# Reading the moving operands of the weight-stream matmuls from the last element to the first

## The reference

```python
h = rmsnorm(x, g_mix)
proj = h @ w_in                  # q, k, v, forget logits, LRU x, LRU gate, memory q, 3 x 2048 merge-gate logits
mk, mv = split(rmsnorm(mem, g_mem) @ w_mem_kv)
...                              # y_fox (causal attention), y_lru (gated recurrence), y_mem (cross-attention)
y_d = einsum('bsnc,ncd->bsnd', branches, w_branch)
x = x + sum(sigmoid(gate_logits + b_gate) * y_d) @ w_out
up = causal_conv3(rmsnorm(x, g_ffn) @ w_ffn_up)
u_act, u_val = split(up)
return x + (gelu(u_act) * u_val) @ w_ffn_down
```

## Time and profile before

| | |
|---|---|
| median of 2 runs | 1644.3 us (1644.13 to 1644.46) |
| the profiled execution's own time | 1643.98 us |
| its span, first to last instruction | 1642.2 us |
| mean granted TensorE clock | 0.998 |
| PE, matmuls | 1628.4 us busy, 8560 instructions |
| PEld, weight loads | 1392.5 us, 8560 |
| DVE | 1050.9 us, 1257 |
| ACT | 870.2 us, 1192 |
| POOL | 25.3 us, 30 |
| DMA | 309.58 MB, mean 189 GB/s |

### The profile page before, as it was taken

One profiled execution on the slowest core, in us unless ns is written; L12 is line 12 of the kernel. 1 busy time (PEld: TensorE's weight loads), 2 busy tenths in 40 slices (PEclk: granted clock), 3 DMA queues, 4 the chain that ended last, 5 costly groups with the idle time before them and its releaser, 6 DMA issues.

```text
span 1642.2 us, 24812 instructions
## 1 busy us (share of the span) xinstructions
PE 1628.4 (99%) x8560; PEld 1392.5 (85%) x8560; DVE 1050.9 (64%) x1257; ACT 870.2 (53%) x1192; POOL 25.3 (2%) x30
## 2 busy tenths in 40 slices
PE   9999999999999999999999999999999999999999
PEld 7778888778888888888888888888888888888887
DVE  6755578656657565564755777777777777544443
ACT  7565667356554545445445655555555555433332
POOL 0000021000000000000000000000000000000000
PEclk9999999999999999999999999999999999999999
DMA  9544455655456556555565556555556555665663
GB/s 347 177 158 153 148 170 195 238 198 167 162 172 192 192 179 193 190 189 185 186 195 182 168 188 204 186 181 195 179 181 202 191 181 190 202 207 192 205 205 116
DMA packets 85280, 309.58 MB, mean 189 GB/s; under 512 B 9832, under 2 KB 10352, under 8 KB 84976
## 3 DMA queue, kind: packets, MB, share of 16 engines
q1 hardware_dynamic: 83952, 303.14, 55.7%
q0 software_dynamic: 1136, 5.78, 1.0%
q10 hardware_dynamic: 144, 0.01, 0.0%
HBM read 306.78 MB, written 2.11 MB: 188 GB/s over the span
## 4 chain that ended last, share of the span: by engine, by line
PE 94%; DVE 2%; DMA 2%; ACT 1%; SPq 0%; issue 0%; ACTq 0%; DVEq 0%
PE psG L359 90%; DMA raw<-w_units 2%; PE psM L359 2%; DVE W L1016 1%; PE psM L444 0%; ACT W L661 0%; DVE normed L1054 0%; PE psM L597 0%; DVE X L1200 0%; PE psM L480 0%; DVE x_n L1296 0%; ACT fox_square L690 0%; PE psM L478 0%; DVE dec_u L1163 0%; ACT L804 0%
## 5 line engine op out<-in xcount | busy, mean ns | idle before, releaser
L1016 DVE TENSOR_TENSOR W<-raw,W 128x1024 fp32r<-128x1024 f32 x566 | 686.6, 1225 | 390.8 <-ACT W L661 388.3
L359 PE MATMUL psG<-X,W 128*128 128x512 f32 (+1 forms) x4864 | 853.1, 337 | 0.0
L359 PEld LDWEIGHTS psG<-X,W 128*128 128x128 f32 x4864 | 741.5, 188 | 108.4
L661 ACT ACTIVATE W<-raw 128x1024 fp32r<-128x1024 f32 x566 | 590.5, 1055 | 402.4 <-PE psG L359 384.7
L359 PE MATMUL psG<-W,hidden 128*128 128x512 f32 x1056 | 239.5, 389 | 0.0
L359 PEld LDWEIGHTS psG<-W,hidden 128*128 128x128 f32 x1056 | 198.2, 188 | 41.0
L359 PE MATMUL psG<-W,X 128*128 128x512 f32 x768 | 180.5, 394 | 0.0
L359 PEld LDWEIGHTS psG<-W,X 128*128 128x128 f32 x768 | 144.5, 189 | 30.3 <-issue 0.4
L669 ACT ACTIVATE low<-psG 128x512 f32<-128x512 f32 x100 | 59.9, 599 | 153.6 <-PE psG L359 153.6
L359 PE MATMUL psG<-Y,W 128*128 x768 | 134.4, 337 | 0.0
L359 PEld LDWEIGHTS psG<-Y,W 128*128 128x128 f32 x768 | 117.0, 188 | 17.1
(11 more groups left out here) (191 smaller groups left out, 551.2 us busy)
## 6 DMA issues: line engine op xcount, KB each, us to landing
raw<-w_units SPq DMA_DIRECT2D x566, 512.0 KB, 3.8
xs<-xT SPq DMA_DIRECT2D x4, 512.0 KB, 8.4
x_tok<-x_rows POOLq DMA_DIRECT2D x1, 2048.0 KB, 13.7
mem_raw<-first_data SPq DMA_DIRECT2D x3, 512.0 KB, 4.8
mem_raw<-memT SPq DMA_DIRECT2D x3, 512.0 KB, 7.5
out<-x_tok POOLq DMA_DIRECT2D x3, 512.0 KB, 4.2
lru_rg<-w_rg POOLq DMA_DIRECT2D x8, 128.0 KB, 4.0
c_all<-c_rows POOLq DMA_DIRECT2D x1, 1024.0 KB, 8.1
```

The source lines that it names most:

```text
L359: return nc.tensor.matmul(*a, skip_group_check=True, **kw)
L661: nc.scalar.activation(W[:, s, :, 0], raw[:, s], ACT.Copy).then_inc(hi_done, 1)
L1016: V.tensor_tensor(W[:, s, :, 1], raw[:, s], f32(W[:, s, :, 0]), ALU.subtract).then_inc(lo_done, 1)
```

## The change

Every matmul of a unit reads its moving operand from the last column to the first. In the narrow groups the activations keep their layout, so the results come out in reverse order and are written backwards into `psG`, which puts each at its old place. In the wide groups the host lays out the 512 columns of each row of a unit backwards; read backwards they are in the old order, and `psG` is written forwards as before. Stationary operands are read as before. The branch loop over n on PE becomes three copies of its body with fixed addresses. The matmuls into `psM` don't change. The diff, whole:

```diff
@@ group
                         for t, ts in enumerate(halves):
-                            mm(psG[:, b + t, :], W[:, s, k, 0, ts], x_hl, start=kt == 0, stop=False)
+                            mm(psG[:, b + t, ::-1], W[:, s, k, 0, ts], x_hl[:, ::-1, ::-1], start=kt == 0, stop=False)
                         for t, ts in enumerate(halves):
-                            ins = mm(psG[:, b + t, T:], W[:, s, k, 1, ts], x_hl[:, 0], start=False, stop=kt == last)
+                            ins = mm(psG[:, b + t, 2 * T - 1:T - 1:-1], W[:, s, k, 1, ts], x_hl[:, 0, ::-1], start=False, stop=kt == last)
+            def wide_weights(s, k, w_part):
+                return W[:, s, 2 * k:2 * k + 2, w_part][:, ::-1, ::-1]
@@ wide_unit
-                            ins = mm(psG[:, b + t, :], x_hl[:, x_part, t * P:t * P + P], W[:, s, 2 * k:2 * k + 2, w_part],
+                            ins = mm(psG[:, b + t, :], x_hl[:, x_part, t * P:t * P + P], wide_weights(s, k, w_part),
@@ quarter
-                with pe.Fori(0, 3) as n:
+                for n in range(3):
                     for w in range(2):
-                        group("branch0", n, w,
-                              lambda kt: Y[:, bass.ds(n, 1), kt].rearrange("p a h t -> p (a h) t"),
-                              {}, per=2, coef=4, before=before)
+                        group("branch0", n, w, lambda kt: Y[:, n, kt], {}, per=2, coef=4, before=before)
@@ the last unit of the down projection
-                        ins = mm(psG[:, 2 + t, :], x_hl[:, x_part, t * P:t * P + P], W[:, s, 2 * k:2 * k + 2, w_part],
+                        ins = mm(psG[:, 2 + t, :], x_hl[:, x_part, t * P:t * P + P], wide_weights(s, k, w_part),
@@ _unit (on the host)
-    rows = w[src][row:row + steps * P, col:col + cols]
-    return rows.reshape(steps, P, cols).transpose(1, 0, 2).reshape(P, steps * cols)
+    rows = w[src][row:row + steps * P, col:col + cols].reshape(steps, P, cols)
+    if cols == 512:
+        rows = rows[:, :, ::-1]
+    return rows.transpose(1, 0, 2).reshape(P, steps * cols)
```

## The result

The changed kernel takes 1672.8 us against 1644.3: ratio 1.0173, 95% interval 1.0129 to 1.0217. It is slower by 28.5 us. The difference is clear of noise; whether it reaches 2% stays unclear, as the interval lies on both sides of that bound. It is on the other side of my forecast of 1555 us.

A forecast was written before the change was run, and what follows sets the result against it. The prediction took PE's matmuls into `psG`, by their distance from one to the next, to bound the kernel: -96 us gained back and +6 that doesn't return, so 1644.0 - 90 + 1 = 1555 us; 8-in-10 range 1540 to 1740 us.

The forecast's parts named there:

- the price of reading and writing backwards: In all matmuls into `psG`: a gain of 67.0 us narrow and 29.0 us wide, together 96 us.
- the 2.3 ns: Time over two clock periods a column in the attention's float32 matmuls, taken as the part of the excess that stays.
- The excess: Time of a unit matmul beyond one clock period a column: 14.2 ns narrow, 13.5 ns wide.
- What is left is the stream itself: In the unit matmuls: wanting a 4-byte column every period loses some 11 ns a matmul, not lost at half rate.
- no direction: Rival, all unit matmuls: opposite order loses the same 11 ns; 1644 to 1659 us, chance 0.32 including a wide-only gain.
- The loop at 0 us: Branch loop on PE: writing it out wins 0 us; instruction fetches, at most 15 us, were taken as 0.
- The layout and the splits: Host layout of the wide groups: same bytes, same number of loads, same splits of 1024 elements, so 0 us.
- the slack in the up projection: ACT's copy-outs wait 1.6 us each for PE, said to cover groups 0.76 us shorter; at most 33 us lost, none taken.
- It is not the weight load: The forget logits load 40 columns instead of 128 and still follow at 231 ns, so the load doesn't cause the excess.
- The slower one: Rival, backwards reads and writes: broken column pairs halve the rate, 2545 or 3098 us; chance 0.23 with its weak form.
- the partial gains: Rivals where one kind of group gains: only the wide ones, 1618 us, or only the narrow ones, 1577 us.
- The rival's weak form: Backwards access in the unit matmuls doubles the excess: +96 us, 1740 us, chance 0.08.

The follow-up runs named there:

- m2: PE alone, no layer: one float32r matmul repeated 32 times a stretch, operands shifted by 0 to 64 elements; 512 columns backwards 233.1 to 236.6 ns, forwards from 226.6.
- e4: The kernel before the change, forward reads, with every buffer but W moved up by 128 bytes (32 elements): 1656.2 against 1642.3 us, ratio 1.0077.
- m1: PE alone, no layer: stretches in the kernel's wide and narrow orders and of one repeated matmul; forwards 226.8 and 174.2 ns, read backwards 233.3 and 176.8.
- e5: The changed kernel with every buffer but W moved up by 128 bytes: 1679.2 us against 1642.1 for the kernel before the change, ratio 1.0224.
- e6: The kernel before the change, forward reads, with X and Y moved by 64 bytes (16 elements) against all other operands: 1637.1 against 1642.1 us, ratio 0.9970.

## Why the prediction was wrong

**The step that failed** is the price of reading and writing backwards. The prediction said: "All but the 2.3 ns comes back", 96 us, and took that end because "it is a matter of how the reads of this stream fall, and the direction shifts exactly that". Measured: +31.5 us in the same rows. Three things in it were different.

- *The excess is in the main a gap, not a rate.* "What is left is the stream itself" is wrong as it was used: 13.1 to 13.5 ns stay at 256, 320, 384 and 512 columns. The narrow and wide rows, 14.2 over at 384 columns on average and 13.5 over at 512, already spoke for a gap; a rate would have lost less on 384. I had both numbers and did not divide them by their columns. Something that is paid once a matmul need not go when its columns are read the other way. What the direction added is a second term, which grows with the columns (-1.3 ns at 256, 6.6 at 512); the forecast gave it no cost.
- *The starting point was a good one.* I counted the direction as a change from "bad" to "unknown". All moving and stationary tiles of the unit matmuls lie at equal offsets modulo 256 bytes, and m2 shows that this is where the forward read has its smallest gap: 226.7 ns, against 229 to 235 at most others. With so many worse places a change of access pattern was more likely to lose than to win.
- *Symmetry was no argument either way.* The rival "no direction" fell too, by 1.7%: the distance has a direction. Its 1644 to 1659 us missed by 14.

**What held.** That PE's distance sets the time and nothing else would move: yes, the two stretches account for the result. The excess needs 4-byte columns at full rate: right, float32 in two passes and bfloat16 stay at 216 ns. The loop at 0 us: right, ratio 0.9998. The layout and the splits: nothing changed there. Whether the slack in the up projection would have covered a gain wasn't put to the test, since nothing got faster.

**What didn't hold beside it.** "It is not the weight load" is wrong as I used it. The place from which the load reads changes the gap (e4, 226.8 to 232.5 ns), and its size does too. The forget logits' 231 ns, which I took to show that a smaller load changes nothing, lie 4 ns above the wide matmuls' 226.8; m1 has 230.0 and 231.7 ns with 64 and 32 stationary columns at equal offsets.

**The rivals.** The slower one named the wrong mechanism: pairs of columns are not broken. Of the partial gains neither came: both groups lost. The backwards write costs nothing: 174.2 ns in m1 with it (L115) and without (L109). The Trainium skill (PSUM — Partial Sum Buffer, Specifications) says that any non-contiguous pattern slows matmuls significantly; for a step of -1 the trace does not agree. It agrees with a sentence in the Trainium skill (Advanced Engine Details and Errata, PSUM Cachelines), that every two consecutive elements should be contiguous, as they are here. That section has the stricter sentence as well, which the prediction left out. The rival's weak form, +96 us, had the right sign at three times the size. The time fell inside the range of 1540 to 1740 only because the range took in that form, and that is luck.

**What stays open.** Why a backwards read has no offset as good as the forward one's best; what the 13 ns are that no offset removes; what makes the excess 16 ns and more at 448 to 508 columns; and why the same matmuls at the same offset hold one distance in one place and another elsewhere (226.9 and 233.3, 173.4 and 176.4, and both 233 and 237 in e5). That moving and weight-load reads wait for each other in the memory would fit that their relative offset counts; no row shows such a wait. A stationary operand read in the other direction wasn't tried.

## What to carry to other kernels

Where a kernel is one long stream of float32r matmuls, measure the distance from start to start, not the duration, and compare the excess over columns / 2.4 GHz at several lengths before you say what it is. Keep moving operands of 512 columns read forwards, and treat the offset between moving and stationary tiles modulo 256 bytes as a parameter: it was worth 3% of a wide matmul (226.7 against 233.5 ns) and 1% of this kernel's narrow ones (172.5 against 174.2), and it costs an allocation offset. PE alone in a small kernel of labelled stretches finds the candidates. It does not rank them safely, since the same stretch gave values 3 to 6 ns apart in two such kernels; the layer itself has to confirm a choice, as e4 and e6 did.

## What the runs showed of the hardware

- At full rate a float32r matmul with 128 stationary columns, read forwards at equal offsets, pays 13.1 to 13.5 ns beyond its columns at 256, 320, 384 and 512 of them, 15.8 to 17.0 at 480 to 508, and 16.0 or 19.6 at 448 (m1, m2); bfloat16, and float32 in two passes, pay 2.5 to 2.7.
- The distance depends on the offset between the operands modulo 64 elements (226.6 to 235 ns for 512 columns forwards, at multiples of 4 elements), and not on how far apart they lie.
- The direction of the innermost moving read counts (+6.7 ns wide, +2.5 ns narrow in the layer), and for a repeated matmul the price grows with the columns, from -1.3 ns at 256 to +6.6 at 512; the order of the outer runs and the direction of the PSUM write don't count.
- Cutting the weight load from 128 to 32 columns makes the gap smaller at +32 (233.3 to 230.4 ns) and larger at offset 0 (226.7 to 231.7).
- The same matmul at the same offsets can hold either of two distances (226.9 or 233.3 ns with the stationary operand at +4), and keeps the one it has to the end of its stretch.
